# Cached pages spread over 16 partitions each, and one of three page loads issued by GpSimd

## The reference

```python
past = pool[pages]                      # 16 pages of 128 rows
full = concatenate([past, rows])
kcb = compress(full[:, 0], ...)         # blocks of 32 rows at a step of 16: gelu(blk @ w1) @ w2
vcb = compress(full[:, 1], ...)
# nsa_queries: scores on kcb -> importance -> the 16 best blocks of 64 rows,
# softmax over them with full[:, 2] and full[:, 3], a window branch, gates
```

## Time and profile before

| | us |
|---|---|
| median of 3 runs (2358.78 to 2371.11) | 2366.75 |
| span of the profiled execution | 2353.0 |
| sequences stage in it, first to last TensorE instruction | about 461 to 1082 |
| TensorE busy in the span | 2122.3 |
| VectorE, ScalarE, GpSimd busy | 754.5, 602.7, 383.3 |

### The profile page before, as it was taken

How to read it: one execution, slowest core, us unless ns; L and a number is a source line. 1 busy time by engine, 2 the same in 40 slices (tenths; PEclk the granted TensorE clock), 3 DMA queues, 4 the chain that set the end, 5 groups by cost and what they waited for, 6 DMA issues and landing times. The chain is left out here.

```text
span 2353.0 us, 34231 instructions
## 1 busy us (share of the span) xinstructions
PE 2122.3 (90%) x12685; PEld 1829.4 (78%) x12685; DVE 754.5 (32%) x1446; ACT 602.7 (26%) x1271; POOL 383.3 (16%) x304
## 2 busy tenths in 40 slices
PE   6999989859668858788999998989999999999998
PEld 5777768637456646656988886869999999999987
DVE  5544334613233213345544445321111111111115
ACT  4211012112232313234544444221220111111112
POOL 0111112201000000000100000213332233223330
PEclk9999989879789979888999998999999999999999
DMA  5220112166545454533000001321111111111122
GB/s 166 89 65 1 37 50 75 43 94 88 65 61 70 73 66 76 78 57 75 1 1 1 1 1 37 107 82 45 45 45 45 46 53 42 47 45 45 51 65 109
DMA packets 170668, 131.86 MB, mean 56 GB/s; under 512 B 12137, under 2 KB 160314, under 8 KB 170226
## 3 DMA queue, kind: packets, MB, share of 16 engines
q1 hardware_dynamic: 170546, 130.24, 25.0%
HBM read 117.85 MB, written 16.55 MB: 57 GB/s over the span
## 5 line engine op out<-in xcount | busy, mean ns | idle before, releaser
L373 PE MATMUL banks<-halves 128*128 128x344 f32 (+4 forms) x5184 | 856.5, 327 | 12.6 <-POOL halves L382 12.6
L373 PEld LDWEIGHTS banks<-halves 128*128 128x128 f32 (+1 forms) x5184 | 821.7, 188 | 43.2 <-issue 7.5
L373 PE MATMUL banks<-hidden 128*128 128x512 f32 (+3 forms) x1512 | 349.5, 387 | 9.0 <-DVE hidden L382 9.0
L382 POOL TENSOR_TENSOR halves<-core,halves 128x1024 fp32r<-128x1024 f32 (+1 forms) x143 | 243.0, 1707 | 642.7 <-ACT halves L378 491.9
L373 PEld LDWEIGHTS banks<-hidden 128*128 128x128 f32 (+1 forms) x1512 | 254.6, 179 | 77.6 <-issue 9.6
L1005 PE MATMUL banks<-arena 128*128 128x254 f32 (+1 forms) x1152 | 253.4, 377 | 11.3 <-ACT arena L1143 6.6
L1005 PEld LDWEIGHTS banks<-arena 128*128 128x128 f32 x1152 | 212.3, 197 | 38.6 <-issue 6.0
L378 ACT ACTIVATE halves<-core 128x1024 fp32r<-128x1024 f32 (+1 forms) x85 | 88.1, 1047 | 389.8 <-PE banks L373 369.6
L1492 PE MATMUL banks<-kept,arena 128*128 128x64 f32 (+1 forms) x1184 | 172.6, 277 | 6.4 <-ACT arena L1524 4.0
L1921 DVE TENSOR_TENSOR core<-banks,core 128x344 f32<-128x344 f32 x66 | 34.1, 517 | 440.7 <-PE banks L373 440.7
L1492 PEld LDWEIGHTS banks<-kept,arena 128*128 128x128 f32 (+1 forms) x1184 | 150.8, 191 | 20.5 <-issue 16.8
(11 more groups left out here) (203 smaller groups left out, 1745.7 us busy)
## 6 DMA issues: line engine op xcount, KB each, us to landing
core<-in_cache_kv SPq DMA_DIRECT2D x128, 128.0 KB
arena<-in_cache_kv SPq DMA_DIRECT2D x256, 64.0 KB
core<-in_w_gate SPq DMA_DIRECT2D x22, 512.0 KB, 3.8
core<-in_w_up SPq DMA_DIRECT2D x22, 512.0 KB, 3.7
core<-in_x_prompt SPq DMA_DIRECT2D x16, 512.0 KB, 3.5
retention<-in_w_in SPq DMA_DIRECT2D x16, 448.0 KB, 6.0
core<-in_w_down SPq DMA_DIRECT2D x16, 448.0 KB, 3.6
core<-out SPq DMA_DIRECT2D x16, 256.0 KB
```

The costliest lines, as they stand in the source:

```text
L373: done = pe.matmul(out, left[a], right[b], start=(first and i == 0), stop=(last and i == 2))
L382: return engine.tensor_tensor(lo, x, hi.bitcast(F32), ALU.subtract)
```

## The change

Three things change together. A page now lands on 16 partitions, 8 rows on each; eight pages fill the 128 partitions, and the other eight go to a second half of each tile. The 16 loads of the selected values are issued by GpSimd, which reads the page table itself; SyncE keeps the other two sets and the small loads. And the order that follows from it is adapted: the prompt's rows are loaded whole by one early DMA, GpSimd does both of their copies (ScalarE did one), the first weights come in 8 loads of a quarter each way instead of 4, TensorE takes `w1` in another order of k, ScalarE reads the turned rows from PSUM with a step of two elements, and VectorE adds the block mask in two halves.

```diff
+HCH = CH // 2
-    m.selk, m.selv = (sel[:, 2048 * i:2048 * i + 2048].rearrange("p (t n) -> p t n", t=CH) for i in range(2))
+    m.selk, m.selv = (sel[:, 2048 * i:2048 * i + 2048].rearrange("p (h t n) -> p h t n", h=2, t=HCH) for i in range(2))
...
-    m.cmpb = x(4096).rearrange("p (t n) -> p t n", t=CH)
+    m.cmpb = x(4096).rearrange("p (h t n) -> p h t n", h=2, t=HCH)
...
         @block.sync
         def _(sp):
-            load_prompt_rows(sp, s, io, m.pool[0:64, 256 * EARLY_ROWS:4096], EARLY_ROWS, CH, "cmp_in")
+            sp.dma_start(m.pages[0:1, :], io.table).then_inc(s["pages_in"], 16)
             for x, done in enumerate(("b_w_first", "b_w_in0")):
-                dst, src = (w.rearrange("p (a k) n -> p a k n", a=2)[:, :, 4 * x:4 * x + 4, :] for w in (m.w1[0], io.w1[0]))
-                for a in range(2):
+                dst, src = (w.rearrange("p (a k) n -> p a k n", a=4)[:, :, 2 * x:2 * x + 2, :] for w in (m.w1[0], io.w1[0]))
+                for a in range(4):
                     sp.dma_start(dst[:, a, :, :], src[:, a, :, :]).then_inc(s[done], 16)
...
                 for pg, page in enumerate(page_of[q]):
-                    sp.dma_start(dst[8 * pg:8 * pg + 8, :, :],
+                    half, at = divmod(pg, NPG // 2)
+                    sp.dma_start(dst[16 * at:16 * at + 16, half, :, :],
                                  io.pool[bass.ds(page, 1), :, :, lo:lo + n].rearrange("a c t n -> (a c) t n")
                                  ).then_inc(s[done], 16)
...
+            def load_blocks(q):
+                if q > NB_SEQ:
+                    return
+                page_of.pop(q - 3, None)
+                page_of[q] = [sp.value_load(m.pages[0:1, x:x + 1], min_val=0, max_val=NPOOL - 1)
+                              for x in range(NPG * (q - 1), NPG * q)]
+                sp.wait_ge(s["b_grouped"], 2 * q)
+                pages(q, m.cmpb, 0, 256, "cmp_in")
+
             for step in STEPS_B:
-                if step + 1 <= NB_SEQ:
-                    page_of.pop(step - 2, None)
-                    at = NPG * step
-                    page_of[step + 1] = [sp.value_load(m.pages[0:1, x:x + 1], min_val=0, max_val=NPOOL - 1)
-                                         for x in range(at, at + NPG)]
-                q = step + 1
-                if q <= NB_SEQ:
-                    sp.wait_ge(s["b_grouped"], 2 * q - 1)
-                    if q == 1:
-                        sp.wait_ge(s["b_first"], 2)
-                    pages(q, m.cmpb, 0, 256, "cmp_in")
                 if step == 0:
+                    load_blocks(1)
                     sp.dma_start(S0, io.state_in).then_inc(s["r_state_in"], 16)
                     sp.dma_start(m.cst, io.const[:, N_LATE:]).then_inc(s["const_in"], 16)
                 elif step == 1:
...
                 q = step - 1
                 if 1 <= q <= NB_SEQ:
                     wait(sp, "pv_done", q - 1)
-                    pages(q, m.selv, 384, 128, "values_in")
...
                     pages(q, m.selk, 256, 128, "keys_in")
...
+                load_blocks(step + 2)
...
+            def load_values(q):
+                page = [pool.value_load(m.pages[0:1, x:x + 1], min_val=0, max_val=NPOOL - 1)
+                        for x in range(NPG * (q - 1), NPG * q)]
+                if q == 1:
+                    pool.wait_ge(s["r_new_state"], 1)
+                wait(pool, "pv_done", q - 1)
+                for pg in range(NPG):
+                    half, at = divmod(pg, NPG // 2)
+                    pool.dma_start(m.selv[16 * at:16 * at + 16, half, :, :],
+                                   io.pool[bass.ds(page[pg], 1), :, :, 384:512].rearrange("a c t n -> (a c) t n")
+                                   ).then_inc(s["values_in"], 16)
+
+            pool.wait_ge(s["cmp_early"], 16)
+            for q in range(NB_SEQ + 3):
+                if q == 1:
+                    pool.wait_ge(s["pages_in"], 16)
+                if q >= 3:
+                    load_values(q - 2)
+                n = CH if q else HCH
+                for kv in range(2 if q <= NB_SEQ else 0):
                     if q:
+                        pool.wait_ge(s["cmp_in"], 16 * NPG * q)
                         pool.wait_ge(s["b_turned"], TURN_AT["kv"[kv], q - 1, 3] + 1)
-                    pool.tensor_copy(m.cmpg[0:n, kv, :, :, :],
+                    pool.tensor_copy(m.cmpg[:, kv, :, 0:n, :],
...
                     for x in range(4):
+                        g, half = divmod(x, 2)
+                        if q or half == 0:
+                            t = HCH * half + 2 * i
...
-                act.activation(m.XT[:, 2 * i:2 * i + 2, :, 0:nch],
-                                   m.banks[:, u % 2, :].rearrange("p (j g c) -> p j g c", j=2, g=2)[:, :, :, 0:nch],
+                act.activation(m.XT.rearrange("p (h j) g c -> p j h g c", h=2)[:, i, :, :, 0:nch],
+                                   m.banks[:, u % 2, :].rearrange("p (g c h) -> p h g c", g=2, h=2)[:, :, :, 0:nch],
                                    ACT.Copy).then_inc(s["b_kept_act"], 1)
...
-    io.pool = cache_kv[0].rearrange("n (c t) s g d -> n c t (s g d)", t=CH)
+    io.pool = cache_kv[0].rearrange("n (c t) s g d -> n c t (s g d)", t=HCH)
```

More of the change, by code:

```diff
@@ L453, in _ @@
                     sp.wait_ge(s["aw_lo"], KT * NCH)
-                    load_prompt_rows(sp, s, io, m.pool[0:64, 0:256 * EARLY_ROWS], 0, EARLY_ROWS, "cmp_early")
+                    load_prompt_rows(sp, s, m, io)
                 if not stored(n):
@@ L768, with load_prompt_rows @@
 SEQS_B = range(NB_SEQ + 1)
[L771 to L777, removed]
+def load_prompt_rows(sp, s, m, io):
+    sp.dma_start(m.pool[:, 0:HCH * 256].rearrange("p (t n) -> p t n", t=HCH),
+                 io.kvp.rearrange("(c t) n -> c t n", t=HCH)[:, :, 0:256]).then_inc(s["cmp_early"], 16)
 def chunks_of(q):
@@ L854, in _ @@
         def _(sp):
-            load_prompt_rows(sp, s, io, m.pool[0:64, 256 * EARLY_ROWS:4096], EARLY_ROWS, CH, "cmp_in")
+            sp.dma_start(m.pages[0:1, :], io.table).then_inc(s["pages_in"], 16)
             for x, done in enumerate(("b_w_first", "b_w_in0")):
-                dst, src = (w.rearrange("p (a k) n -> p a k n", a=2)[:, :, 4 * x:4 * x + 4, :] for w in (m.w1[0], io.w1[0]))
-                for a in range(2):
+                dst, src = (w.rearrange("p (a k) n -> p a k n", a=4)[:, :, 2 * x:2 * x + 2, :] for w in (m.w1[0], io.w1[0]))
+                for a in range(4):
                     sp.dma_start(dst[:, a, :, :], src[:, a, :, :]).then_inc(s[done], 16)
-            sp.dma_start(m.pages[0:1, :], io.table).then_inc(s["pages_in"], 16)
             for kv in range(2):
@@ L908, in _ @@
                     wait(sp, "pv_done", q - 1)
-                    pages(q, m.selv, 384, 128, "values_in")
                     sp.dma_start(m.winv, io.wins[q - 1, :, :].rearrange("(p t) n -> p t n", t=4)[:, :, 128:256]
-                                 ).then_inc(s["values_in"], 16)
-                    sp.dma_start(m.vcb[q % 2][127:128, :], io.kvs[q - 1:q, 384:512]).then_inc(s["values_in"], 16)
+                                 ).then_inc(s["last_values_in"], 16)
+                    sp.dma_start(m.vcb[q % 2][127:128, :], io.kvs[q - 1:q, 384:512]).then_inc(s["last_values_in"], 16)
                 q = step
@@ L919, in _ @@
                                  ).then_inc(s["keys_in"], 16)
+                load_blocks(step + 2)
         @block.gpsimd
         def _(pool):
[L923 to L929, removed]
+            def load_values(q):
[17 more added lines that the diff above has]
+                for kv in range(2 if q <= NB_SEQ else 0):
                     if q:
+                        pool.wait_ge(s["cmp_in"], 16 * NPG * q)
                         pool.wait_ge(s["b_turned"], TURN_AT["kv"[kv], q - 1, 3] + 1)
-                    pool.tensor_copy(m.cmpg[0:n, kv, :, :, :],
-                                     m.cmpb[0:n, :, P * kv:P * kv + P].rearrange("p t (g d) -> p g t d", g=2)
-                                     ).then_inc(s["b_grouped"], 1)
+                    pool.tensor_copy(m.cmpg[:, kv, :, 0:n, :],
+                                     m.cmpb.rearrange("p h t n -> p (h t) n")[:, 0:n, P * kv:P * kv + P]
+                                     .rearrange("p t (g d) -> p g t d", g=2)).then_inc(s["b_grouped"], 1)
             prepare_attention(pool, s, m)
@@ L940, in position_bias @@
             def position_bias(kv):
-                pe.wait_ge(s[f"b_w_in{kv}"], 48 if kv else 64)
+                pe.wait_ge(s[f"b_w_in{kv}"], 48 if kv else 96)
                 for k in range(16):
@@ L974, in compress @@
                 nb = nch - 1
-                if q or kv:
-                    pe.wait_ge(s["b_grouped"], 2 * q + kv)
+                pe.wait_ge(s["b_grouped"], 2 * q + kv + 1)
                 def turn_rows(i):
@@ L980, in turn_rows @@
                     free_turn_bank(pe, u)
-                    if q == 0 and kv == 0:
```

(29 more changed lines are left out.)

## The result

The changed kernel takes 2213.18 us (median of 4 runs, 2210.89 to 2214.66), the kernel before 2363.38 on the same chip (4 runs, 2358.78 to 2371.11): ratio 0.9378, 95% interval 0.9333 to 0.9423. The forecast was faster, 2244 us, range 2222 to 2315. The profiled execution spans 2211.6 us instead of 2353.0, and took 2213.31.

What follows compares the result with a forecast made beforehand. Page loads on 8 partitions were taken to bound the sequences stage. 30 us at the beginning and 93 over five periods make 123 off 2366.75: 2244 us, range 2222 to 2315.

Steps and rivals of the forecast that it cites:

- What bounds the kernel: Sequences stage: loads of pages on 8 partitions, at 57 GB/s, set the beat of 67.75 us per sequence.
- The rate: Page loads on 16 partitions: 114 GB/s, twice 57, so rows to compress take some 20.5 us with landing, not 37.8.
- Rival C: Page loads: the pages themselves are the limit, so the rate and the period of 68 stay; 2360 us, chance 0.07.
- The period: Sequences stage, steps 3 to 8: 49.2 us instead of 67.75, saving 93 us over five periods.
- GpSimd's chain: GpSimd, each step: wait for `pv_done`, 16 issues, then copy L932; period the larger of 48.4 and 24.9 + 16 d + 1.9.
- d: Time per load issue on GpSimd: 1.4 us, between 0.85 and 1.87; it counts in the period from 1.35.
- A: The forecast: pages about twice as fast, TensorE or GpSimd just beside it sets the pace; 2244 us, 2225 to 2265, chance 0.60.
- B: GpSimd's issues become the bound at 1.6 to 2.3 us each; 2291 us at 1.9, 2319 at 2.2; chance 0.23.
- D: Slower: each load holds GpSimd over 2.7 us, by descriptors or VectorE, between `pv_done` and L932; 2405 us at 3.09; chance 0.10.
- The beginning: Up to sequence 3: first keys issued near 555, not 570.05; sequence 3's copy at 601 instead of 631.29, 30 us off.
- The distance from span to time: The three runs' median lies 13.75 us above the profiled span; this distance was kept, 2230 becoming 2244 us.
- The rest: ScalarE's stepped PSUM copies, the mask in two halves, the prompt's copies and transposes: nothing taken; ScalarE at most 5.4 us.

Runs made afterwards that it cites:

- first experiment: The changed kernel with the values issued by SyncE again, pages still on 16 partitions: 2208.33 us, ratio 0.9454 to the kernel before.
- second experiment: The kernel before with the values issued by GpSimd, pages still on 8 partitions: 2316.24 us, ratio 0.991 to the kernel before.

## Why the prediction was partly right

**What bounds the kernel: right.** The gain comes with the width of the page loads alone (first experiment); with narrow pages a second issuer is worth 0.9% of the time (second), with wide ones nothing.

**The rate: right, and for the reason given.** 114 GB/s forecast, 121 measured; 20.5 us a set forecast, 19.2 measured (564.87 to 584.05). Rival C, the page as the limit, is excluded by 251 GB/s from the same pages. By the paces above, twice the engines at the same pace is just what the step from 8 to 16 does. One thing was missed in it: an issue got cheaper too, 564 ns instead of 677 (medians of lines 872 and 874), so SyncE had more room than thought.

**The period: right in size, the last part by luck.** 49.2 forecast, 49.0 measured. TensorE's 48.4 was taken from the trace of before and is nearly right (48.2 in the undisturbed steps with the values on SyncE). The 0.8 on top of it was to be GpSimd's chain with d = 1.4; what is there is the wait of 0.65 to 0.96 us for L1311, which the prediction didn't have. The chain's form holds (four times the issues), but at d = 0.61 it ends 11.7 us before it would count.

**d: mis-sized, with little effect.** I took 1.4 between 0.85 and 1.87; it is 0.61, below my lower bound. SyncE's 0.85 was the issue for 8 partitions (on 16 it is 0.74), and I took GpSimd to be no quicker than SyncE; it is, on 8 partitions too (10.55 us for 16 issues in the second experiment, 0.66). Below 1.35 d doesn't count: the first copy is done at 626.47, 11.7 us before TensorE's next step. So A's sum stood, and B and D, a third of the chances, were ruled out by a number that no trace of before had. The 2.0 us that the Trainium skill ("DMA: Bandwidth & Descriptors", Anatomy of one DMA) gives are no issue time either: a load by GpSimd lands 3.9 us (median) after it was issued, but the next issue follows after 0.61.

**The beginning: the step that failed.** "The first keys, issued at 570.05 now, go out near 555": I moved that time by the 15 us by which the constants were to come sooner, and carried over the 33.8 us between the retention step's start and the keys. Both halves were wrong, the first by 7 us and the second by 8, and in both a small load stands behind page loads in SyncE's queue. The retention step, which waits for the constants, starts at 514.24 instead of 536.28, 22.0 us sooner and not 15: SyncE reached the first pages at 487.01, where I had 490.2, and the step begins 13.8 us after the issue of the constants instead of 26.6. And the 33.8 us measured 25.5 (514.24 to 539.73), for in them stood a wait that belongs to the page loads: SyncE sends out the retention output, 16 KB, and reads it back when it has arrived. In the kernel before:

```profile
554.71 0.52 SPq L883 DMA_DIRECT2D ret_out<-core  x1
559.11 0.55 SPq L885 DMA_DIRECT2D out<-arena  x1
569.55 0.31 SPq L887 DMA_DIRECT2D core<-ret_out  x1
```

14.8 us from L883 to L887, and the pages ahead of it in the same queue had landed at 569.44 (GpSimd's copy). With GpSimd alone on narrow pages the two times are 555.88 and 555.75. With wide pages the set has landed at 528.08, before the 16 KB go out, and the reading back follows 5.0 us later (4.95 and 4.97 with 128 and 32 partitions). No run moves the small load by itself; that the queue makes the wait is read from these five traces. So the keys go out at 539.73, the rows of sequence 3 at 564.87 instead of 579, and TensorE enters step 3 at 589.24 straight from its own work, where I had it wait until 603. That is 14 us of the 31 by which the time was missed.

**The distance from span to time: 12 us of the 31.** I kept the 13.75 us between the profiled span and the median of three runs. In the changed kernel an execution takes 1.7 us more than its span (2213.31 and 2211.6). The other 12 were no overhead: the profiled execution of before was a quicker one than the three runs shown. In every run of the study whose span is on record the time is 1.6 to 3.4 us above the span, so that execution took about 2355 us, an estimate. The 12 us are near the 13 by which the stages behind differ between profiles, but no other execution of the kernel before was profiled. That kernel scatters, 2310.78 to 2371.11 over all runs of this study; the changed one stays within 2207.89 to 2222.72. A fixed addition was the wrong form.

**The end: 5 us.** Nothing was taken for it; the last steps lose their wait for the first keys (1.8 us), and TensorE enters step 8 without having stood still, so that the part up to the probabilities takes 17.65 us (834.38 to 852.03) instead of 21.30.

**The rest: right.** ScalarE's copies from PSUM with a step of two take 600 ns (598 before); the waits for them are 7.1 us (6.6).

## What to carry to other kernels

A DMA share of 0.51 was a full queue: each load went to 8 partitions, half of the DMA engines had nothing (the share is 1.01 with 16), and the other half were held to 57 GB/s by the partitions they wrote (from 32 partitions on, the same share moves 2.5 times as much). Look at the partitions that one load touches before asking who issues it or how large its pieces are. When a duration is carried over from the old trace, look at what stood ahead in the same queue in that time, for it goes away with the load that is made faster. Add the distance between span and time from the same execution, or state it as scatter. And when one engine slows another, look in the timelines at what ends when the slow instruction ends, before you name the cause: here it was not the new issues but the old copy that they had moved.

## What was not expected of the hardware

Issuing a load depends on its shape. Medians on SyncE are 677 ns for 8 partitions of 16 rows, 564 for 16 of 8 and for 32 of 4, and 333 for 128 of one; on GpSimd 594, 528 and (128 partitions) 537. GpSimd's issues are here no dearer than SyncE's, but for those to 128 partitions.

The disturbance between GpSimd and VectorE went the other way than rival D had it: GpSimd's issues kept their 528 ns (longest 688), and VectorE waited. The Trainium skill ("SBUF — State Buffer", Who interferes with whom) says that whichever of the two starts first holds the ports they share until it is done, and names `tensor_scalar` among the kinds that can collide and reduces among those that can't. The trace agrees in three of the five steps: the copy L945 started 0.11 us before L1311 and took its usual 1.90 us, and the `tensor_scalar` of 8x127, 0.27 us otherwise, ended 0.08 us after it. In the other two L1311 started 0.19 us before the copy, during GpSimd's last issue, and still ended only after the copy (2.18 us); by the order of the starts it should not have waited for it.
